# The first feed-forward product by seven products too, ahead of the second, with the weights' low parts on VectorE

## The reference, cut to what matters

```python
        h2 = modulate(rmsnorm(x, norm_mlp_g[l]), shift2, scale2)
        y = jnp.square(jax.nn.relu(h2 @ w_ff1[l])) @ w_ff2[l]
        x = x + gate2 * y
```

## Time and profile before

| what | value |
|---|---|
| median of 3 runs | 2276.47 us (2276.26 to 2278.19) |
| span of the profiled execution | 2274.7 us, the page gives no other time for it |
| PE busy | 2224.7 us (98%), 10292 matmuls |
| PEld / DVE / ACT / POOL busy | 82% / 66% / 38% / 54% |
| granted TensorE clock, mean | 0.992 |
| feed-forward part | 946.8 us to the end |

### The profile page before, as it was taken

How to read it: one execution, slowest core, us unless ns; L and a number is a source line. 1 busy time by engine, 2 the same in 40 slices (tenths; PEclk the granted TensorE clock), 3 DMA queues, 4 the chain that set the end, 5 groups by cost and what they waited for, 6 DMA issues and landing times.

```text
span 2274.7 us, 26399 instructions
## 1 busy us (share of the span) xinstructions
PE 2224.7 (98%) x10292; PEld 1859.0 (82%) x10292; DVE 1508.9 (66%) x1506; ACT 859.9 (38%) x1152; POOL 1224.3 (54%) x521
## 2 busy tenths in 40 slices
PE   6999999999998999999999999999999999999999
PEld 6888888888887878888888888888888888888887
DVE  5876976775646687446687677678666556656756
ACT  5435454533356222333333333333333333333331
POOL 2004344342521455267776766777776667676763
PEclk9999999999999999999999999999999999999999
DMA  9966355454636687444443444343433333333342
GB/s 348 319 219 227 127 184 192 146 201 164 240 130 238 245 286 269 141 127 134 130 126 128 128 128 132 121 149 111 130 111 102 108 96 102 112 94 107 101 170 102
DMA packets 185465, 365.52 MB, mean 161 GB/s; under 512 B 15354, under 2 KB 40444, under 8 KB 183296
## 3 DMA queue, kind: packets, MB, share of 16 engines
q1 hardware_dynamic: 176992, 340.79, 45.5%
q10 hardware_dynamic: 8352, 23.07, 2.7%
HBM read 332.33 MB, written 31.48 MB: 160 GB/s over the span
## 4 chain that ended last, share of the span: by engine, by line
PE 87%; DVE 6%; issue 2%; DMA 2%; ACT 1%; POOL 1%; SPq 1%; DVEq 0%; ACTq 0%; POOLq 0%
PE ps L852 19%; PE ps L853 19%; PE ps L854 19%; PE ps L1345 8%; PE ps L1344 8%; PE ps L1346 8%; DVE acc L1967 1%; DMA araw<-in_w_ada 1%; PE ps L886 1%; PE ps L913 1%; PE ps L1142 1%; DVE acc L2018 1%; DVE rt L2278 1%; DVE qn L2270 0%; SPq L459 0%
## 5 line engine op out<-in xcount | busy, mean ns | idle before, releaser
L396 POOL TENSOR_TENSOR wlo<-wraw,whi 128x1024 fp32r<-128x1024 f32 (+3 forms) x112 | 280.8, 2519 | 465.4 <-ACT whi L391 438.3
L844 POOL TENSOR_TENSOR wlo<-wq,whi 128x1024 fp32r<-128x1024 f32 x150 | 387.0, 2582 | 123.6 <-ACT whi L1859 123.6
L844 POOL TENSOR_TENSOR wlo<-wraw,whi 128x1024 fp32r<-128x1024 f32 x132 | 381.2, 2888 | 33.8 <-ACT whi L1859 33.8
L852 PE MATMUL ps<-h2T,whi 128*128 128x512 f32 x1024 | 398.6, 389 | 0.0
L854 PE MATMUL ps<-h2T,wlo 128*128 128x512 f32 x1024 | 398.4, 389 | 0.0
L853 PE MATMUL ps<-h2T,whi 128*128 128x512 f32 x1024 | 398.3, 389 | 0.0
L2612 DVE TENSOR_TENSOR yacc<-ps,yacc 128x1024 f32<-128x1024 f32 x202 | 246.4, 1220 | 215.9 <-PE ps L1346 213.2
L1344 PE MATMUL ps<-whi,ahi 128*128 128x512 f32 x840 | 326.9, 389 | 0.2 <-DVE yacc L2612 0.2
L1346 PE MATMUL ps<-whi,alo 128*128 128x512 f32 x840 | 326.8, 389 | 0.0
L1345 PE MATMUL ps<-wlo,ahi 128*128 128x512 f32 x840 | 326.8, 389 | 0.0
L1859 ACT ACTIVATE whi<-wq 128x1024 fp32r<-128x1024 f32 x150 | 159.1, 1060 | 354.1 <-PE ps L854 223.3
(11 more groups left out here) (340 smaller groups left out, 3995.4 us busy)
## 6 DMA issues: line engine op xcount, KB each, us to landing
araw<-in_w_ada SPq DMA_DIRECT2D x144, 512.0 KB, 5.8
wraw<-in_w_ff SPq DMA_DIRECT2D x136, 512.0 KB, 3.8
wq<-in_w_ff SPq DMA_DIRECT2D x120, 512.0 KB, 4.2
wraw<-in_w_in SPq DMA_DIRECT2D x72, 512.0 KB, 5.8
arawx<-in_w_ada SPq DMA_DIRECT2D x48, 512.0 KB, 4.7
wraw<-in_w_out SPq DMA_DIRECT2D x32, 512.0 KB, 7.0
xnat<-in_x ACTq DMA_DIRECT2D x4, 1024.0 KB, 8.5
xT_d<-xT ACTq DMA_DIRECT2D x1, 4096.0 KB, 13.3
```

Of the source, the lines that this page charges most:

```text
L396: pool.tensor_tensor(wlo[:, slot, 0:kb, 0:cols], wraw[:, slot, 0:kb, 0:cols], whi[:, slot, 0:kb, 0:cols].bitcast(F), ALU.subtract).then_in ...
L844: pool.tensor_tensor(wlo[:, slot, :, :], raw, whi[:, slot, :, :].bitcast(F), ALU.subtract).then_inc(lo_ready, 1)
L852: pe.matmul(dst, lhs[0], rhs[0], start=start, stop=False)
```

## The change

The first product of chunks 1 to 15 is done by the seven-product method too, and all of it stands ahead of the second product. One pass over 14 blocks is called a group (`group_order`): seven products q0 to q6 of two blocks each (i = 0, 1).

- Groups 0 to 14 (`GROUPS_A`, "group A" below) make chunks 1 to 15 of the first product. A block is now 24 matmuls with 256 columns (`ff1_block`). The moving operands are sums of quarters of h2 (`comb`), made once. q0, q2, q3 and q4 use PSUM bank 0, q1 and q5 bank 1, q6 bank 2; q2 to q5 are added on top of what the bank holds, and between two of them the bank is read out (`bank_copy` on ACT, `bank_add` on DVE).
- Chunk 0's blocks "F" stay as they were, in order ahead of group 0.
- The activations, their sums and their low parts (`a_high`, `a_total`, `a_low`) go through four slots (`ring`) to DRAM (`a_store`, from ACT's queue to `a_d`), and come back by `comb_load`.
- Groups 15 to 30 ("group B") are the second product. A group takes two chunks (the first two groups one), so that a product has two blocks of 12 matmuls with 512 columns and one `add_product` per product. q0, q2, q3 and q4 use banks 0 and 1, q1 and q5 banks 2 and 3, q6 banks 4 and 5; q2 to q5 are added on top of what the banks hold.
- The low parts of weights move from POOL to DVE (`weight_low`), but those of q6 (`POOL_LOWS`) stay on POOL, and so do those of chunk 0.

At step s of a group (the slot of a block, 0 to 13), ACT makes the high part of the block three places on, and DVE the sums for the block three places on and the low part of the block two places on. The rest of a step comes behind these on the same engine. The diff, cut to this:

```diff
+GROUPS_A = CHUNKS - 1
+GROUPS = GROUPS_A + CHUNKS
+def group_order(g):
+    w = [[("W", g, q, i) for i in range(blocks_of(g))] for q in range(PRODUCTS)]
+    if g < LAST:
+        return sum(w, [])
...
+        def ff1_block(g, q, i):
+            bank = 2 if q == 6 else 1 if q in (1, 5) else 0
...
+            if i == 0:
...
+                elif q == 2:
+                    pe.wait_ge(f_copy, 3 * g + 1)
+                elif q == 3:
+                    pe.wait_ge(f_copy, 3 * g + 3)
+                elif q == 4:
+                    pe.wait_ge(f_add, 3 * g + 1)
...
+            for m in range(2):
+                dst = ps[:, bank, 256 * m:256 * m + 256]
+                for t in range(4):
...
+                    pe.matmul(dst, w[0][:, c], hi, start=new, stop=False, skip_group_check=True)
+                    pe.matmul(dst, w[0][:, c], lo, start=False, stop=False, skip_group_check=True)
+                    ins = pe.matmul(dst, w[1][:, c], hi, start=False, stop=t == 3, skip_group_check=True)
...
+        def ff2_block(g, q, i):
...
+                elif q == 2:
+                    pe.wait_ge(f_added, 7 * gb + 1)
+                elif q == 3:
+                    pe.wait_ge(f_added, 7 * gb + 3)
+                elif q == 4:
+                    pe.wait_ge(f_added, 7 * gb + 4)
...
+        def step_hi(p):
+            if p + 3 < len(FF_ORDER):
+                ff_hi(FF_ORDER[p + 3])
...
+        def a_store(c, q):
+            act.wait_ge(a_lo, PRODUCTS * c + order.index(q) + 1)
+            act.dma_start(a_d[:, c, q, :, :], ring[:, slot, :, :]).then_inc(a_stored[slot], 16)
...
+            for s in range(14):
+                step_hi(first + s)
+                if s in (2, 4, 6):
+                    bank_copy(g, (s - 2) // 2)
...
+                    elif s == 2:
+                        a_high(c, 0)
+                        a_store(c, 6)
...
+                    elif s == 4:
+                        a_high(c, 3)
+                        a_store(c, 1)
...
+        def weight_low(key):
+            dve.wait_ge(hi_ready, n + 1)
+            dve.tensor_tensor(wlo[:, slot, :, :], raw, whi[:, slot, :, :].bitcast(F), ALU.subtract
+                              ).then_inc(f_low, 1)
...
+        def a_total(c, q):
+            dve.wait_ge(a_stored[slot], STORED_0 + 16 * uses)
...
+                step_forms(first + s)
+                step_low(first + s)
...
+                    elif s == 2:
+                        a_low(c, 0)
+                        a_total(c, 2)
+                        a_total(c, 3)
+                        a_low(c, 1)
+                    elif s == 3:
+                        gate2_step(gate2_at(g, 0))
+                    elif s == 4:
+                        a_total(c, 5)
+                        a_low(c, 2)
+                    elif s == 5:
+                        a_low(c, 3)
...
+                if s == 8:
+                    bank_add(g, 3)
...
+                step_forms(p)
+                step_low(p)
...
+                elif key[0] == "W" and key[2] and key[3] == 0:
+                    add_product(g, key[2] - 1)
```

More of the change, by code:

```diff
@@ L115 @@
 PRODUCTS = 7
[L116 to L139, removed]
@@ L150, in raw_place @@
[L150 to L156, removed]
+POOL_LOWS = [key for key in FF_ORDER if key[0] == "W" and key[2] == 6]
+POOL_AT = {key: N_FF + GB + i + 1 for i, key in enumerate(POOL_LOWS)}
+LO_AT = {key: i + 1 for i, key in enumerate(key for key in FF_ORDER[GB:] if key not in POOL_AT)}
+FORM_AT = {}
+for _p, _key in enumerate(FF_ORDER):
+    if _key[0] == "W" and _key[2] in (1, 2, 4):
+        for _t in {1: (1, 3), 2: (2,), 4: (4,)}[_key[2]]:
+            FORM_AT[_t, _key[1], _key[3]] = len(FORM_AT) + 1
@@ new lines, in bank_copy @@
+        def bank_copy(g, q):
+            act.wait_ge(blk_done, FF_AT["W", g, q, 1] + 1)
+            bank = ps[:, 1 if q == 1 else 0, :].rearrange("p (m n) -> p m n", m=2)
+            if q == 1:
+                if g:
+                    act.wait_ge(a_lo, PRODUCTS * g + 1 if g < CHUNKS - 1 else 0)
+                    act.wait_ge(a_sum, 4 * g + 1)
+                dst = quad(cb, 1, 1)
+            else:
+                if g:
+                    act.wait_ge(f_add, 3 * (g - 1) + (3 if q == 0 else 2))
+                dst = tt[:, q // 2, :, :]
+            act.activation(dst, bank, ACT.Copy).then_inc(f_copy, 1)
@@ new lines, in _ @@
+        p0 = GB + 14 * GROUPS_A
+        for p in range(p0, len(FF_ORDER)):
+            step_hi(p)
+            if p == p0:
+                a_store(CHUNKS - 1, 2)
+                a_high(CHUNKS - 1, 1)
+            elif p == p0 + 1:
+                relu_of(GROUPS_A - 1, 6)
+            elif p == p0 + 2:
+                a_high(CHUNKS - 1, 0)
+                a_store(CHUNKS - 1, 1)
+            elif p == p0 + 4:
+                a_store(CHUNKS - 1, 0)
+            if FF_ORDER[p] == ("W", LAST, 2, 1):
+                act.wait_ge(y_T, 1)
+                act.activation(x3[:, :, :], ps[:, 4:8, :], ACT.Copy).then_inc(y_act, 1)
@@ L2579, in form @@
+        dve.tensor_tensor(comb_raw(5), u(0, 1), comb_raw(2), ALU.subtract).then_inc(s_sum, 1)
+        dve.wait_ge(blk_done, FF_AT["F", 0, 3] + 1)
+        dve.tensor_tensor(comb_raw(3), u(0, 0), u(1, 0), ALU.subtract).then_inc(s_sum, 1)
+        def form(t, g, i):
+            slot = FF_AT["W", g, t, i] % RING
+            b11, b12, b22, b21 = [piece(r, i) for r in range(4)]
+            uses = g + 1 - (2 if i == 1 and g > GROUPS_A + 1 else 0)
+            if t == 1:
                 for r in (0, 1):
-                    dve.wait_ge(wq_loaded[r], 16 * (h + 1))
@@ new lines, in step_forms, with step_low, slot_of @@
+        def step_forms(p):
+            if p + 3 < len(FF_ORDER):
+                key = FF_ORDER[p + 3]
+                if key[0] == "W" and key[2] in (1, 2, 4):
+                    for t in {1: (1, 3), 2: (2,), 4: (4,)}[key[2]]:
+                        form(t, key[1], key[3])
+        def step_low(p):
+            if p + 2 < len(FF_ORDER) and FF_ORDER[p + 2] not in POOL_AT:
+                weight_low(FF_ORDER[p + 2])
+        def slot_of(c, q):
+            place = PRODUCTS * c + (RING_OF[q] if c < CHUNKS - 1 else (3, 2, 1, 0).index(q))
+            return place % 4, place // 4
```

875 lines of the change are left out of this document (544 added, 331 removed).

## The result

| | before | after |
|---|---|---|
| median | 2276.4 us (2274.8 to 2278.2, 4 runs) | 2542.0 us (2539.1 to 2543.9, 4 runs) |
| span of the profiled execution | 2274.7 us | 2540.5 us |
| mean granted clock | 0.992 | 0.953 |

The changed kernel takes 1.1163 times as long (95% interval 1.1147 to 1.1179). The forecast was 2547 us in 2455 to 2625.

A forecast was written before the change was run, and what follows sets the result against it. PE, busy 98% of the span, was taken as the bound. First product +141, second +122 and the turn +8 make 271 us on a span of 2274.7, 2545.7; as median 2547 us, range 2455 to 2625.

The forecast's parts named there:

- turn to group 0: From chunk 0 to group 0: first low parts come late, 13 us in all, group 0 gives 5 back; + 8 (0 to 20).
- PE's price: First product: 256-column matmuls 0.1196 us apart, so PE needs 40.2 us per group A against 43.5 per chunk before.
- The rival of the weight loads: Group A: weight loads limit 256-column matmuls to 0.156 us instead of 0.1196; 105 us more, 2652 us; 4%.
- the chain: Group A: DVE's work delays q4's second sum, then ACT's high part and read-out; q3 starts at T+27.15 instead of T+17.2.
- landing term: Group A: DVE's `a_total(3)` waits for the store of q6's activation, issued at T+11.5, landing after 3.6 us (2.6 to 5.8).
- The rival of the quick landings: Group A: landings quick or already in, DVE's own chain decides; 48.7 or 47.5 for 51.2, 2508 us; 15%.
- Block 5's wait: Group A: PE wants block 5's low part at T+14.35, gets it at T+17.5 and idles 3.3 us.
- The sign that went with the term: In the changed profile, DVE's short sums into `ring` show idle time ahead, ended by a DMA.
- The clock: Behind q3's wait the granted clock falls to 0.50 for 3.3 us, costing 1.65 us in each of 29 groups.
- The rival that the clock holds: Groups A and B: no fall of the clock behind q3's waits; 48 us less, 2499 us; 12%.
- The other side: Hand-overs hidden, PE never kept: 2226 us, 3%; against it, q4's second sum keeps group A at 44.5 us at best.
- The "some 5" us for POOL's holds: Turn from chunk 0 to group 0: part of the 24 us of work ahead of group 0's first low part.

The follow-up runs named there:

- filling the waits: Changed kernel plus matmuls that nobody needs ahead of q3's wait, 44 of 256 columns in groups A, 12 of 512 in groups B but the last: 2481.7 us.
- with turns: Changed kernel with products reordered so another bank's blocks stand between those of one bank, group B's load order and group A's end changed: 2325.6 us.

## Why the prediction was right, step by step

The direction, the mechanisms and their places were right. Two terms were off by as much as each other in opposite directions (22 us too much, 22 too little), so that the sum is nearer than its parts: that 2547 lies within 5 us of 2542 is luck. (PE's busy share is 90%, for the 87% forecast.) Measured against 43.5 us for a chunk and 631.9 us for all that follows before (1327.9 us from 946.8 to the end, less 16 x 43.5):

| term | forecast | measured |
|---|---|---|
| first product, 15 groups A | +141 | +119.4 (771.9 us from 993.2 to 1765.1, for 652.5) |
| second product and end | +122 | +143.5 (775.4 us for 631.9) |
| turn to group 0 | +8 | +2.9 (PE's idle time there is 3.32) |
| sum | +271 | +265.8 |

**PE's price: right.** 256-column matmuls start 0.12 us apart:

```profile
1303.72 0.28 PE L1416 MATMUL ps<-hc,whi 128*128 128x256 f32 x1
1303.84 0.28 PE L1417 MATMUL ps<-hc,whi 128*128 128x256 f32 x1
1303.96 0.28 PE L1418 MATMUL ps<-hc,wlo 128*128 128x256 f32 x1
```

The rival of the weight loads falls. The estimate of 109 ns by the formula of the Trainium skill ("TensorE: Matmul & The Clock Gate", section "Back-to-back issue gap"), which the page gives for a matmul in isolation, is again below the 120 ns that the trace has.

**Group A: the chain was right, its landing term wrong.** T is 1304.5: the last matmul of the first five blocks starts at 1318.72, the next could have at 1318.84, less 5 x 2.87. Forecast and measured, after T: the high part of q0's activation ended 11.5 and 11.4; the store of q6's activation issued 11.5 and 9.5; `a_total(3)` 15.1 and 12.6; block 5's low part ready 17.5 and 15.0; `a_total(5)` 20.0 and 17.3; q4's second sum ended 25.4 and 22.8; q3 27.15 and 24.5. So up to T+11.5 the chain is as forecast, and from `a_total(3)` on all is 2.5 to 2.7 us early. The step that failed: "At T+11.5 ACT issues the store of q6's activation. DVE's `a_total(3)` writes to that slot of `ring`, so it waits for the landing." ACT's queue issued the store at 1313.97, ahead of the start of the two ACTIVATEs that stand before it in the program (1314.76 and 1315.23), and the three stores from 1314.0 to 1318.4 landed after 2.6 to 2.7 us, not 3.6:

```profile
DMA to landing us min/median/max: 2.6/2.6/2.7
```

So it was in when DVE came to it at 1317.10, and of the 3.6 us 2 went by the earlier issue and 1 by the quicker landing. The rival of the quick landings (15%), which takes out the same 2.5 us, holds for this term. Block 5's wait was 0.58 and not 3.3, for the same reason. The sign that went with the term did not show either: outside group 0 DVE's short sums waited for a store only four times, 0.2 to 0.5 us.

**The clock: mechanism right, size wrong.** The forecast took a fall of 3.3 us from the one in the earlier trace rows and charged 1.65. Here PE mostly works 5 to 6 us at 0.50 behind q3's wait; filling the waits gives 2.4 us in A and 2.7 in B. In A the clock took 0.8 more and the landings 2.6 less, which makes 51.1 of 52.9; in B the error of the clock counts in full. The rival that the clock holds falls; the experiment with filled waits shows what it would have given.

**Group B: waits right.** 3.9, 1.6 and 0.8 forecast, 3.78, 1.41 and 0.46 measured. 46.1 forecast and 47.5 measured, of which the clock is 1.05. The two short groups, from 1765.1 to 1819.6, lost 8.2 us each and not 4.8; PE's waits in them are 5.5 and 5.8 us, the rest was not taken apart.

**The turn: right only as a sum.** PE waits 3.3, 1.3 and 0.5 us for the first low parts, 5 us and not 13. But group 0 gives nothing back: it lasts 55.6 us (993.2 to 1048.8), 4.4 more than the other groups A on average, which the table counts in the first row. The "some 5" us for POOL's holds had no row behind them; here DVE's two sums beside POOL took 4.49 and 4.39 us for 2.29 alone, 4.3 in all.

**The other side: the argument held, its floor nearly so.** It said that q4's second sum alone keeps a group A at 44.5 us or more in this order. With the read-out ahead of the high parts 43.9 was reached, with turns 43.7 on average, which is no less than a chunk took before.

**What the forecast had not priced:** the second gate step and a low part ahead of `bank_add`, hidden behind q3's late start. Only taking the first wait away brought them up.

## What to carry to other kernels

When products are added up in one bank, the engine that frees the bank sets the time: put its read at the head of its step, and work of another bank between the two products. Add to a long hand-over what the clock costs behind it: here 2.4 to 2.7 us on top of waits of 3.8 to 6.3. And when a wait is taken away, look at once at what stands ahead of the next hand-over, since it has been hidden until then.

## What the runs showed of the hardware

- A DMA on ACT's queue was issued 0.8 and 1.3 us before the start of the ACTIVATEs that stand ahead of it in the program (1313.97 against 1314.76 and 1315.23). Where the ACTIVATE ahead of it waited for PE, the issue came only after that one had started (1334.57 behind 1334.54).
- Waits of 1.41 us in groups B, and of 0.9 to 1.8 in groups A, left the granted clock at 1.00; waits of 3.78 and 6.27 us were followed by 0.50, and PE mostly worked at it for 5 to 6 us, in three groups B for 2.6 to 3.4.
- Matmuls that nobody needs, in place of the wait, kept the clock at 0.99 to 1.00 and made the kernel 60 us faster.
- A DVE instruction beside one of POOL's subtractions of 1024 elements took 2.2 us longer (3.43 for 1.22, 2.88 for 0.69), and DVE would have needed 1.13 us for the subtraction itself.
